# An expert loop with eight adjacent weight rows to a partition: 32x32 block transposes on VectorE in place of TensorE's, and a last down product by token group

## What is computed

```
xn = rmsnorm(x, ffn_norm_w)
logits = xn @ w_router + b_router
top_val, top_idx = top_k(logits, 4);  gates = softmax(top_val)
# for each expert e, over the tokens that chose it:
hid = x_blk @ w_gate_up[e] + b_gate_up[e]          # w_gate_up[e]: 1024 x 2048
gate = minimum(hid[:, :1024], 7.0)
up = clip(hid[:, 1024:], -7.0, 7.0)
glu = gate * sigmoid(1.702 * gate)
y = ((up + 1.0) * glu) @ w_down[e] + b_down[e]     # w_down[e]: 1024 x 1024
x = x + sum over the token's experts of its gate * y
out = rmsnorm(x, final_norm_w)
```

## Time and profile before

| | us |
|---|---|
| median of 3 runs | 1515.26 |
| lowest, highest | 1512.69, 1515.73 |
| the profiled execution | 1512.43 |
| its span | 1510.7 |

### The profile page before, as it was taken

One profiled execution on the slowest core, in us unless ns is written; L12 is line 12 of the kernel. 1 busy time (PEld: TensorE's weight loads), 2 busy tenths in 40 slices (PEclk: granted clock), 3 DMA queues, 4 the chain that ended last, 5 costly groups with the idle time before them and its releaser, 6 DMA issues.

```text
span 1510.7 us, 33686 instructions
## 1 busy us (share of the span) xinstructions
PE 1369.0 (91%) x13162; PEld 633.5 (42%) x13163; DVE 565.8 (37%) x1174; ACT 301.8 (20%) x566; POOL 368.6 (24%) x434
## 2 busy tenths in 40 slices
PE   6997989879899999999999999988988988889982
PEld 3444555555433444343433444433433433334441
DVE  2888888553522223322232212332222223222231
ACT  3122323131301212121211112211111111112122
POOL 4001111010221232331342223232223223222323
PEclk9999999979969999999999999999999999999996
DMA  9211000300387999999999999999999999999974
GB/s 301 79 66 56 1 29 1 148 21 18 125 312 298 375 382 388 399 410 406 408 399 409 405 410 409 405 408 401 401 410 403 407 405 399 399 404 406 401 302 139
DMA packets 109974, 451.10 MB, mean 299 GB/s; under 512 B 18264, under 2 KB 36852, under 8 KB 77142
## 3 DMA queue, kind: packets, MB, share of 16 engines
q1 hardware_dynamic: 86566, 427.88, 70.8%
q0 software_dynamic: 20304, 21.03, 6.1%
q10 hardware_dynamic: 3072, 1.76, 0.5%
HBM read 439.05 MB, written 17.17 MB: 302 GB/s over the span
## 4 chain that ended last, share of the span: by engine, by line
PE 61%; DMA 20%; DVE 10%; SPq 4%; ACT 2%; issue 2%; POOL 0%; ACTq 0%; DVEq 0%; POOLq 0%
PE bank L1869 28%; DMA ring<-in_w_gate_up_dram 19%; PE bank L1905 12%; PE bank L1552 5%; PE bank L1719 4%; PE bank L1931 3%; DVE dslots L1007 2%; SPq L380 2%; SPq L375 2%; PE bank L1836 1%; DVE qkbuf L1031 1%; PE bank L1854 1%; PE bank L1618 1%; PE bank L1547 1%; PE bank L1825 1%
## 5 line engine op out<-in xcount | busy, mean ns | idle before, releaser
L1869 PE MATMUL bank<-ring,wq 128*32 128x512 f32 x5184 | 590.0, 608 | 49.3 <-DMA ring<-in_w_gate_up_dram 46.4
L1869 PEld LDWEIGHTS bank<-ring,wq 128*32 128x32 f32 x5184 | 163.7, 112 | 425.2 <-issue 424.5
L1905 PE MATMUL bank<-dslots,intra 128*32 128x256 f32 x5056 | 286.0, 380 | 0.0
L1905 PEld LDWEIGHTS bank<-dslots,intra 128*32 128x32 f32 x5056 | 157.8, 110 | 108.6 <-issue 11.1
L887 ACT ACTIVATE wq<-bank 128x512 f32<-128x512 f32 x128 | 66.1, 602 | 632.3 <-PE bank L1869 632.3
L561 POOL DMA_INDIRECT acc_rows<-rows,idx_out x83 | 151.0, 1819 | 46.2 <-POOL idx_out L551 28.3
L1431 DVE TENSOR_TENSOR intra<-bank,small 128x256 f32<-128x256 f32 x128 | 45.4, 417 | 293.1 <-PE bank L1931 293.1
L1552 PE MATMUL bank<-hbuf,ring 128*128 128x512 f32 x320 | 147.7, 603 | 0.0
L1360 DVE TENSOR_REDUCE small<-bank 128x4 f32<-128x8 f32 x34 | 5.7, 167 | 343.9 <-PE bank L1825 343.9
L551 POOL COPY idx_in<-idx 128x4 int32 (+1 forms) x34 | 6.3, 186 | 456.9 <-PE bank L1836 405.7
L556 POOL DMA_INDIRECT wq<-xn_rows,idx_in x88 | 91.9, 1044 | 49.7 <-POOL idx_in L551 29.3
(11 more groups left out here) (267 smaller groups left out, 1040.6 us busy)
## 6 DMA issues: line engine op xcount, KB each, us to landing
ring<-in_w_gate_up_dram SPq DMA_DIRECT2D x256, 1024.0 KB, 21.3
dslots<-in_w_down_dram SPq DMA_DIRECT2D x124, 1024.0 KB, 24.5
ring<-in_w_in_dram SPq DMA_DIRECT2D x12, 1024.0 KB, 12.1
ring<-in_w_out_dram SPq DMA_DIRECT2D x4, 1024.0 KB, 4.8
ring<-in_w_down_dram SPq DMA_DIRECT2D x4, 1024.0 KB, 20.5
rows<-in_x_dram SPq DMA_DIRECT2D x4, 512.0 KB, 6.6
hbuf<-in_x_dram SPq DMA_DIRECT2D x4, 512.0 KB, 4.6
xn_rows<-convbuf POOLq DMA_DIRECT2D x4, 512.0 KB, 4.2
```

Source lines behind the costliest of these rows:

```text
L1869: ins = M(bank[g][GROUP * j:GROUP * (j + 1), :], xT[:, g, c % 2, (c // 2) * GROUP:(c // 2 + 1) * GROUP], w[:, :, j * QD:(j + 1) * QD], sta ...
L1905: ins = M(b[GROUP * j:GROUP * (j + 1), col:col + QD], actT[:, g, c % 2, (c // 2) * GROUP:(c // 2 + 1) * GROUP], w[:, cc, j * QD:(j + 1) * QD],
```

## The change

1. Weight rows are laid to partitions in another order: partition p now holds rows 8p to 8p+7. Slot c of gate/up is row 8p + c of each partition, so a partition's run is still 8 KB, and the runs are 64 KB apart in device memory. A down slot is rows 8p + 2u and 8p + 2u + 1, one run of 8 KB.
2. A contraction chunk c is then the features 8p + c. Since a quarter of 256 features is 32 x 8, a 32x32 block transpose of every eighth column inside a quarter brings feature 8(32j + r) + c to partition 32j + r. DVE does that: `xt_turn` reads `xg`, `hid_turn` reads the gate/up banks in PSUM. PE's transposes, ACT's copies `hid_copy` and `xT_copy`, and the semaphores `xt_done`, `ht_done` and `half_read` go. The bias of gate/up is transposed to the same order (`bias_turn`).
3. PE's loop body is gate/up of visit i, then the whole down product of visit i-1. It waits for `hid_ready` (banks read) and `xt_ready` ahead of gate/up.
4. The last visit's down product is written per group instead of per slot, into banks 0 to 3, in the order 0, 2, 3, 1. Each group has a semaphore; ACT and POOL copy and scatter group by group (`LAST_ORDER`, `d_last`, `y_last`).

```
 sync:
+                src = w_gate_up[0, e].rearrange("(p c) n -> p c n", c=KC)[:, c, :]
+                sp.dma_start(view(ring, c * SLOT, SLOT), src).then_inc(slot_in[c], 16)
+            def down_rows(e, u):
+                return w_down[0, e].rearrange("(p c) n -> p c n", c=KC)[:, 2 * u:2 * u + 2, :]
...
 gpsimd, ahead of the last scatters:
-            pool.wait_ge(y_ready, m + 3)
-            pool.sem_inc(pool_step, 1)
             fetch_rows(idx_out, (E - 1) % STAGES, m * 2 + 6)
-            for g in range(GROUPS):
+            for n, g in enumerate(LAST_ORDER):
+                pool.wait_ge(y_last, n + 1)
+                pool.sem_inc(pool_step, 1)
                 scatter(g)
...
 scalar, end:
-            act.wait_ge(d_used, m * 4 + 12)
             act.wait_ge(landed, m + 2)
-            results((E - 1) % STAGES)
+            for g in LAST_ORDER:
+                act.wait_ge(d_last[g], 1)
+                A(yb[:, g, :], bank[g][:, 0:QD], ACT.Copy,
+                  scale=slot_gate[:, (E - 1) % STAGES, g:g + 1]).then_inc(y_last, 1)
...
 vector:
+            def xt_turn(visit):
+                dve.wait_ge(gathered, visit * (16 * GROUPS))
+                V.transpose(xT.rearrange("p g (c s) -> p g c s", c=KC),
+                            xg.rearrange("p g (r c) -> p g c r", c=KC)).then_inc(xt_ready, 1)
...
+            def hid_turn(visit):
+                dve.wait_ge(gu_used, visit * KC)
+                for g in range(GROUPS):
+                    V.transpose(hidT[:, g, :, :].rearrange("p h (c s) -> p h c s", c=KC),
+                                bank[g][:, :].rearrange("p (h r c) -> p h c r", h=2, c=KC)).then_inc(hid_ready, 1)
...
                 lower(e3)
+                hid_turn(i + 1)
+                xt_turn(i + 2)
                 act_part(i % E, i + 1, base + STEPS_IDX)
...
 tensor, loop:
                 pe.wait_ge(hid_ready, i * GROUPS)
+                pe.wait_ge(xt_ready, i + 1)
                 gate_up(i)
-                pe.wait_ge(idx_ready, i + 3)
-                xt_turn(i * (16 * GROUPS) + 32 * GROUPS)
                 pe.wait_ge(act_ready, i)
                 pe.wait_ge(y_ready, i)
                 tokens = tokens_left(pe, i - 1)
-                down(i - 1, tokens, (0, 1))
-                pe.wait_ge(xt_ready, i + 2)
-                hid_turn(i, 0)
-                down(i - 1, tokens, (2, 3))
-                pe.wait_ge(half_read, i * 2 + 1)
-                hid_turn(i, 1)
+                down(i - 1, tokens)
...
 tensor, end:
+            for u in range(4):
+                pe.wait_ge(slot_in[u], m * 16 + 80)
+            def last_down(g):
+                for c in range(KC):
+                    w = view(ring, (c // 2) * SLOT, 2, D)[:, c % 2, :]
+                    for j in range(4):
+                        ins = M(bank[g][GROUP * j:GROUP * (j + 1), 0:QD],
+                                actT[:, g, c * GROUP:(c + 1) * GROUP],
+                                w[:, j * QD:(j + 1) * QD], start=(c == 0), stop=(c == KC - 1))
+                ins.then_inc(d_last[g], 1)
```

156 lines of the change are left out of this document (60 added, 96 removed).

## The result

| | before | after |
|---|---|---|
| median, us | 1515.28 | 1497.09 |
| lowest, highest | 1512.69, 1515.73 | 1496.63, 1497.92 |
| the profiled execution | 1512.43 | 1496.78 |
| its span | 1510.7 | 1495.0 |

The ratio is 0.9881, with a 95% interval of 0.9862 to 0.9901: the changed kernel is faster by 18.2 us in the medians, where 9.2 were forecast. The two profiled executions lie 15.7 us apart. The other 2.5 us come from before's profiled execution, which lay 2.85 us under its median, while the one of after lies 0.3 under its own.

The account below looks back on a forecast made before the run. It took weight transfers to bound the loop, with PE setting the pace in the first four visits. PE's 6.2 us less the opening's 4.1 gave 2.1, plus 7.1 from the tail: 9.2 us earlier, 1506 us, range 1493 to 1520.

Parts of the forecast that it names:

- The transfers' rate: Weight transfers in the expert loop: no change of rate from the new row layouts; each per cent worth 10.2 us.
- Rival (b): Weight transfers: the rate rises since a down slot makes 128 runs instead of 256; 1496 us at 1%; chance 0.14.
- The sign by which the prediction wanted to be judged: Steady loop: periods staying at 32.7 us would show it right, a difference over 0.3 us either way wrong.
- PE's transposes: Expert loop: taking 3.1 us a visit off PE returns at most 6.2 us, in the opening visits only.
- PE's first wait for a slot: Expert loop: PE waits for slots from about the seventh visit, 142 us in all in place of 46.
- The opening: Ahead of the loop: DVE's first xT transpose delays the bias additions, so gate/up starts 4.1 us later.
- DVE's new work: Each visit: four transposes at 0.71 us and one at 1.2 to 1.4, about 4.2 together, adding nothing on the end.
- Rival (c), the clock: Expert loop: PE's new slot waits lower its clock, costing 8 us, 1514 us; chance 0.10 together with (d), the tail gaining less.
- The tail: After the loop: first copy waits for visit 30's scatters; read-back 9.2 us earlier, 7.1 of it from the tail.
- The base: Whole time: the profiled execution's 1512.43 minus 9.2 gives 1503.2; adding 2.83 to reach the median gives 1506.1.

Follow-up runs that it names:

- e3: The changed kernel with only the down slots read as before (256 pieces of 4 KB, not 128 of 8 KB): 1505.28 us, ratio 0.9943 to before.
- e4: The changed kernel with both down and gate/up slots read as before: 1507.59 us, ratio 0.9950 to the kernel before.
- e8: The changed kernel with PE's three batches of eight transposes per visit put back as work nobody reads: 1502.90 us, ratio 0.9911 to before.
- e5: The kernel before with only the down slots' rows in the new layout, one 8 KB run per partition: 1509.35 us, ratio 0.9963 to before.
- e6: The changed kernel with DVE's first transpose of x behind the third bias addition instead of ahead of all: 1490.34 us, ratio 0.9837 to before.
- e9: The changed kernel with DVE's four 128x512 gate/up transposes done twice in each visit: 1498.12 us, ratio 0.9880 to before.
- e1: The changed kernel run again without any edit: 1499.18 us, ratio 0.9895 to before.
- e2: The changed kernel with gate/up slots read as before, 128 adjacent rows without the 64 KB step: 1498.59 us, ratio 0.9888 to before.
- e7: The changed kernel with the last down product, copies and scatters again slot by slot in before's order: 1496.91 us, ratio 0.9878 to before.

## Why the prediction was right in direction and short in size

It said 1506 us; the time is 1497.09, inside the range of 1493 to 1520. Step by step:

**The transfers' rate: the step that failed.** "I take no change of rate" was wrong, and so was the ground for it, that "neither length limits it visibly". Rival (b), whose mechanism is that a down slot makes 128 runs instead of 256, is what happened: -7.6 us by e3 and e4 against a row of 1004.3, 0.75% of the loop, and its own figure was 1496 at one per cent. I gave it 0.14 because the slices "show no split". They can't: a visit's eight gate/up and four down slots all lie within one slice of 37.8 us. By the measured cost a down slot of 4 KB pieces takes 128 x 0.5 ns = 0.06 us more than one of 8 KB, of some 2.7 us a slot, 2.4%, and the same rows swing between 366 and 421 GB/s with and without a scatter. The trace of before gave no evidence for equal rates; I took the absence of a pattern for one. For the case that it was made for, no change of rate, the sum came close: e4 is the changed kernel with the old layouts, and took 1507.59 us, 0.9950 of before, where the sum has 1506 and 0.994. The sign by which the prediction wanted to be judged did show it. From gate/up of visit 18 to that of visit 31 a visit took 32.43 us (1004.79 to 1426.36), 0.32 under the 32.75 of before, just over the limit of 0.3 that it had set.

**PE's transposes: right, and a little too large.** Expected -6.2 us, all of it in the opening visits; e3 and e4 against before give -5.3, and e8 the same 5.4 from the other side. That it buys nothing in the later visits holds at the old rate; at the new one it may buy more, as the trace of e5 has it, with 3.6 us for 7.6. The windows of the third and fourth visit show the mechanism: 406 and 407 GB/s for 376 and 395. PE's first wait for a slot is at 632.27, in the seventh visit, as forecast. These waits sum to 92.9 us, with 7.9 more from 600 us on that the profile lays to "issue" at the same line, and not to 142. Two things took the rest: the loop is 12.2 us shorter, and the gate/up products themselves took 23.8 us longer (613.8 for 590.0 us busy), in part at a lower clock.

**The opening: right.** Expected +4.1, measured +4.55. The gathers landed 9.8 us after B (423.18) and not 10.1, and the transpose took 2.00 us and not 1.3. PE's gap of 5.89 us names the addition that it waits for. e6 proves the cause by moving the transpose alone.

**DVE's new work: price partly wrong, cover right.** 0.685 us for a 128x512 transpose from PSUM was inside the taken 0.71. The 128x1024 one, whose source takes every eighth element, took 2.05 us mean and not 1.2 to 1.4. That made little difference to the loop: e9 laid another 80 us there for some 3.

**Rival (c), the clock: small, and at one place.** The granted clock between 1000 and 1400 fell from 0.98 to 0.95. The pair of slots that starts at 1441.05 took 5.25 us behind a wait of 2.68, where before took 3.64 behind 1.17. Its window, with the clock as the third figure from the end:

```profile
1441.05:1446.30 5.25, 5.25 (x36) 1.39 (x40) 0.00 (x0) 0.00 (x0) 0.00 (x0) 0.69 0.66 269
```

The first 1.95 us of it read 0.50, the lower level of 1.2 GHz; before's last pair reads 1.00. It is the last pair, nothing follows that would hide it, and so A to D is 1.50 us longer. The wait just ahead does not decide alone: in e3 the pair behind 2.20 us took 3.64, in e6 5.34. From 600 us on, 14 of the 41 pairs of slots that two groups use behind a wait for their landing were slow (5.10 to 5.34 us), this one among them. The 13 others can be paid out of the wait for the next slots; that they cost nothing is argued and not tried. In the trace of before it was 4 of 23 such pairs, and not only the one that the prediction names. The Trainium skill (TensorE: Matmul & The Clock Gate, HAM oscillation) describes a kernel that loses at every wait for a slice; the trace agrees for those 14 pairs, and not for the 27 others.

**The tail: mechanism right, size short by one term.** First copy behind the landing of visit 30's scatters, 10.6 us after the end of its results: forecast 10.6, measured 1469.07 - 1458.47 = 10.6. First scatter after D: forecast 1477.7 - 1453.5 = 24.2, measured 24.37, so 6.91 us sooner than before, where the sum has 7.1. What I missed: the scatters and their landing were taken "as before", 8.35 us, but the order 0, 2, 3, 1 puts a group with tokens last (10 of them, by the 40 packets of 1 KB that this scatter moves). From the last issue to the read-back it is 3.7 us (1476.12 to 1479.84); before, with the empty group 3 last, 2.7 (1492.55 to 1495.27). So 9.35 and -5.91 in place of -7.1.

**The base.** The sum was carried from before's profiled execution to its median by adding 2.83. In the changed kernel the distance was 0.31. By e1 the stages ahead of the loop alone vary by 7.9 us between executions of one kernel, so this carry-over is uncertain by a few us, and the range had no term for it.

Sum of the parts by the runs: opening +4.55, PE -5.3, pieces -7.6, last pair +1.5, tail -5.9, together -12.8, and -3.4 of chance ahead of the loop makes -16.1, against 15.4 in the two traces; the 0.7 between them is the distance of after's S to A from 1004.3.

## What to carry to other kernels

Where transfers pace a loop, count the contiguous pieces, not the bytes alone: choose which rows share a partition so that a partition's rows are adjacent and one transfer reads them in one piece. A slice or window that mixes two kinds of transfer says nothing on the rate of either; if the sum hangs on that rate, take the equality as unknown and give both signs their weight. When a step moves from one engine to another, look at its very first instance: ahead of the loop it may stand with nothing beside it, and here the order of two steps on DVE was worth 6 us there.

## What the runs showed of the hardware

- **A piece costs 0.5 ns on 16 engines, between 4 and 8 KB.** Two contrasts: 4 to 8 KB in the down slots, 0.51 ns; 8 to 4 KB in gate/up, 0.51. The step from 8 to 16 KB gives 0.50, but it halves the transfers as well, so there the price of a piece is not shown by itself. If the pieces are spread evenly, it is 8 ns of one engine a piece (16 x 0.5, an estimate), in transfers of 1 and 2 MB that come out at 401 to 412 GB/s between 1000 and 1400 us. The Trainium skill (DMA: Bandwidth & Descriptors, Why small descriptors are slow) speaks of a fixed overhead of about 3 cycles a packet, and gives a 256-byte one as its example; by its fabric clock of 850 MHz that is 3.5 ns, an estimate. The 8 ns estimated from the runs are more than twice that, and they count at 4 KB, where the page holds joining descriptors to packets worth it at 256 bytes and below only. The measurement decides.
- **A step of 64 KB between partitions costs nothing** (e2: 1004.71 us against 1003.56 to 1005.06).
- **A block transpose with every eighth element of SBUF as source** takes 2.05 us in the mean for 128x1024 (2.00 at 423.18, 2.09 at 1448.81); 128x512 from PSUM, every eighth element too, takes 0.685, and with plain steps in SBUF 0.711.
- **The stages ahead of the loop vary by 8 us** between executions of the same instructions (B at 412.98 to 421.23 in the profiles of the changed kernel and its variants, and at 413.64 to 421.23 in e1 to e4, which ran on one chip). The cause was not looked for.
- **An indirect scatter with only empty rows lands about 0.7 to 1.1 us sooner** than one with 10 tokens: from its issue to the release of the reader it is 2.7 us in the three traces where the empty group 3 is last (before, e5, e7) and 3.4 to 3.8 us in the eleven where group 1 is last.
